# Second block of a two-block transformer: the dilated branch's projections placed around the latent norms and ahead of the up-projections

## What is computed

```python
h = rmsnorm(x, attn_norm[l])
c_q, c_kv, k_r, q_d, k_d, v_d = split(h @ w_in[l])      # 384, 256, 32, 512, 512, 512 columns
o_a = mla_mixer(c_q, c_kv, k_r, ...)                    # latent branch
    # q  = rmsnorm(c_q) @ w_uq   -> 8 heads x 96
    # kv = rmsnorm(c_kv) @ w_ukv -> 8 heads x (64 + 64)
    # per-head rmsnorm of q and k (96 wide), rope on the last 32, dense attention
o_b = dilated_attention(rmsnorm(q_d), rmsnorm(k_d), v_d, rel_bias)   # 8 heads x 64, per-head norm
x = x + concat(o_a, o_b) @ w_out[l]
x = x + conv_ffn(rmsnorm(x, ffn_norm[l]), ...)
```

## Time and profile before

| | |
|---|---|
| time, 3 runs | 2110.36, 2115.12, 2116.67 us, median 2115.12 |
| span of the profiled execution | 2111.4 us |
| its own time | not given apart from the span; the span lies 3.7 us below the median |
| busy: PE / PEld / DVE / ACT / POOL | 92% / 77% / 52% / 40% / 13% |
| mean granted TensorE clock | 0.953 |
| DMA | 254.93 MB, mean 121 GB/s |

### The profile page before, as it was taken

How to read it: one execution, slowest core, us unless ns; L and a number is a source line. 1 busy time by engine, 2 the same in 40 slices (tenths; PEclk the granted TensorE clock), 3 DMA queues, 4 the chain that set the end, 5 groups by cost and what they waited for, 6 DMA issues and landing times.

```text
span 2111.4 us, 31880 instructions
## 1 busy us (share of the span) xinstructions
PE 1948.4 (92%) x12326; PEld 1628.3 (77%) x12326; DVE 1107.7 (52%) x2071; ACT 843.1 (40%) x1579; POOL 283.1 (13%) x194
## 2 busy tenths in 40 slices
PE   5799999999999998998779997979899988799998
PEld 2595555758888887993379997867899987778998
DVE  0523433464344345334556556186687744858785
ACT  1323334343323234223434444345455434545453
POOL 1200000110000012100000001230323113213221
PEclk9899999999999999999889998889999988899999
DMA  9313333433333332413435663440465534224663
GB/s 271 110 61 120 112 108 120 139 91 99 97 98 95 100 99 91 120 61 129 129 83 160 184 181 102 123 125 1 122 190 172 157 90 145 81 61 138 180 182 100
DMA packets 405876, 254.93 MB, mean 121 GB/s; under 512 B 8064, under 2 KB 404640, under 8 KB 405728
## 3 DMA queue, kind: packets, MB, share of 16 engines
q1 hardware_dynamic: 404576, 249.19, 39.9%
q0 software_dynamic: 1152, 3.71, 0.7%
HBM read 251.75 MB, written 1.11 MB: 120 GB/s over the span
## 4 chain that ended last, share of the span: by engine, by line
PE 83%; DVE 9%; ACT 3%; issue 2%; DMA 2%; POOL 2%; SPq 0%; DVEq 0%; ACTq 0%; POOLq 0%
PE bank L1685 59%; PE bank L1664 8%; PE bank L1767 5%; PE bank L1784 5%; PE bank L1776 3%; DVE WORK L1453 2%; PE bank L1735 1%; DVE TOK L1594 1%; ACT parts L1055 1%; DMA raw<-ada_w 1%; PE bank L1762 1%; DVE parts L882 1%; POOL parts L882 1%; DVE TOK L1589 1%; POOL WORK L1007 1%
## 5 line engine op out<-in xcount | busy, mean ns | idle before, releaser
L1685 PE MATMUL bank<-AT,parts 128*128 128x256 f32 (+1 forms) x4656 | 689.6, 310 | 29.3 <-DVE AT L868 16.2
L1685 PEld LDWEIGHTS bank<-AT,parts 128*128 128x128 f32 x4656 | 639.0, 194 | 79.6 <-issue 29.6
L1055 ACT ACTIVATE parts<-raw 128x1024 fp32r<-128x1024 f32 (+1 forms) x368 | 368.1, 1040 | 327.8 <-PE bank L1685 316.3
L882 DVE TENSOR_TENSOR parts<-raw,parts 128x1024 fp32r<-128x1024 f32 (+2 forms) x300 | 416.0, 1412 | 151.7 <-ACT parts L1055 151.1
L1685 PE MATMUL bank<-HID,parts 128*128 128x256 f32 (+1 forms) x2592 | 399.8, 316 | 9.1 <-DVE HID L1401 9.1
L1685 PEld LDWEIGHTS bank<-HID,parts 128*128 128x128 f32 x2592 | 367.2, 192 | 39.9 <-DVE HID L1401 9.7
L1685 PE MATMUL bank<-parts,AT 128*128 128x256 f32 (+1 forms) x2208 | 285.0, 291 | 35.2 <-POOL parts L882 19.1
L1685 PEld LDWEIGHTS bank<-parts,AT 128*128 128x128 f32 x2208 | 279.2, 200 | 42.0 <-issue 28.5
L882 POOL TENSOR_TENSOR parts<-raw,parts 128x1024 fp32r<-128x1024 f32 x68 | 169.0, 2493 | 510.8 <-ACT parts L1055 510.6
L1664 PE MATMUL bank<-raw,CS 128*2 128x256 f32 x768 | 180.3, 390 | 22.4 <-DMA CON<-const 12.4
L1664 PEld LDWEIGHTS bank<-raw,CS 128*2 128x2 f32 x768 | 63.1, 86 | 126.3 <-issue 40.0
(11 more groups left out here) (145 smaller groups left out, 1360.0 us busy)
## 6 DMA issues: line engine op xcount, KB each, us to landing
raw<-mlp_w SPq DMA_DIRECT2D x128, 512.0 KB, 4.0
raw<-ada_w SPq DMA_DIRECT2D x96, 512.0 KB, 4.6
raw<-w_up SPq DMA_DIRECT2D x88, 512.0 KB, 4.7
raw<-w_in SPq DMA_DIRECT2D x32, 512.0 KB, 4.8
raw<-w_down SPq DMA_DIRECT2D x32, 512.0 KB, 4.0
raw<-odd_w_in SPq DMA_DIRECT2D x24, 512.0 KB, 3.6
raw<-w_out SPq DMA_DIRECT2D x16, 512.0 KB, 3.6
raw<-even_w_in SPq DMA_DIRECT2D x12, 512.0 KB, 4.1
```

Source lines behind the costliest of these rows:

```text
L882: ng.tensor_tensor(chunk_part(c, 1), chunk_raw(c), chunk_part(c, 0).bitcast(F32), ALU.subtract)\
L1055: return nc.scalar.activation(o, i, ACT.Copy)
L1685: ins = MM(out, stay, move, start=kt == 0 and i == 0, stop=kt == kts - 1 and i == 2)
```

## The change

In `plan()` the second block's layer gets another order:

- `dil` 0 stands directly behind the latent projections; then come `stat cq` and `stat ckv`; then `dil` 1, 2, 3; then the seven up-projections `mq` and `mkv`; then `dil` 4 and 5.
- the `post` units: `dq` behind `dil` 1, `dk` behind `dil` 3, `mq` behind the up-projections (ahead of `dil` 4), `mk` behind `dil` 4.
- the 4 `turn` units of the dilated branch come ahead of the 8 of the latent branch, and the jobs of kind N ahead of those of kind M.
- ACT squares the five latent tiles at the end of its part of `latent` 2, no longer in the two `stat` units; so it does that ahead of draining `dil` 0.

By the rule above the splits of the dilated chunks move too: those of `dil` 0 go behind `latent` 1, of `dil` 1 behind `latent` 2 (behind the squares), of `dil` 2 behind `stat ckv`, of `dil` 3 behind `dil` 1, the four chunks of `dil` 4 and 5 behind `mq` 1, `mq` 2, `mkv` 0 and `mkv` 1 (where those of `dil` 0 and 1 stood before). Those of `w_out_2` stay behind `dil` 4 and 5.

The rope tables of the first block shrink to one copy of a head's 64 columns: `CON` goes from 1744 to 976 columns. DVE reads them with a broadcast over the heads; the product with the sine is written as four instructions a unit, one for each half and block of tokens, where it was two.

```diff
@@ plan(), second block @@
         for n in range(3):
             pan = panel("w_in_2", l, 0, KT, n * PW, PW if n < 2 else 160)
             add("latent", ("latent", l, n), layer=l, n=n, panel=pan)
-        norm("cq", l, N, "g_cq", src="CQ", dst="CQ", kts=QLT)
-        norm("ckv", l, N, "g_ckv", src="CKV", dst="CKV", kts=KVT)
-        for n in range(3):
-            pan = panel("w_uq_2", l, 0, QLT, n * PW)
-            add("mq", ("mq", l, n), layer=l, n=n, panel=pan)
-        for n in range(4):
-            pan = panel("w_ukv_2", l, 0, KVT, n * PW)
-            add("mkv", ("mkv", l, n), layer=l, n=n, panel=pan)
         for n in range(6):
+            if n == 1:
+                norm("cq", l, N, "g_cq", src="CQ", dst="CQ", kts=QLT)
+                norm("ckv", l, N, "g_ckv", src="CKV", dst="CKV", kts=KVT)
+            if n == 4:
+                for m in range(3):
+                    pan = panel("w_uq_2", l, 0, QLT, m * PW)
+                    add("mq", ("mq", l, m), layer=l, n=m, panel=pan)
+                for m in range(4):
+                    pan = panel("w_ukv_2", l, 0, KVT, m * PW)
+                    add("mkv", ("mkv", l, m), layer=l, n=m, panel=pan)
+                add("post", ("post", l, "mq"), what="mq", layer=l)
             pan = panel("w_in_2", l, 0, KT, 672 + n * PW)
             add("dil", ("dil", l, n), layer=l, n=n, panel=pan)
-            for what in {0: ("mq",), 1: ("mk",), 3: ("dq",), 4: ("dk",)}.get(n, ()):
+            for what in {1: ("dq",), 3: ("dk",), 4: ("mk",)}.get(n, ()):
                 add("post", ("post", l, what), what=what, layer=l)
+        for part in "qk":
+            for i in range(2):
+                add("turn", ("turn", 2 + l, "d" + part, i), layer=2 + l, ft=("d" + part, i))
         for part in "qk":
             for i in range(4):
                 add("turn", ("turn", 2 + l, "m" + part, i), layer=2 + l, ft=("m" + part, i))
-        for part in "qk":
-            for i in range(2):
-                add("turn", ("turn", 2 + l, "d" + part, i), layer=2 + l, ft=("d" + part, i))
-        attention([job(kind=k, layer=2 + l, h=h, b=b, keys=256) for k in "MN" for h in range(8) for b in range(TB)])
+        attention([job(kind=k, layer=2 + l, h=h, b=b, keys=256) for k in "NM" for h in range(8) for b in range(TB)])
@@ ACT, unit "stat" @@
-                    if x.src != "H":
-                        settle()
                     for kt in range(x.squared, x.kts):
@@ ACT, unit "latent", n == 2 @@
+                        settle()
+                        for name in ("cq", "ckv"):
+                            st = index[("stat", name, x.layer)]
+                            for kt in range(st.kts):
+                                square(pos, st, kt)
@@ DVE, unit "tok" with rope @@
-                        step(V.tensor_tensor(pick(r, half), pick(src, 1 - half), pick(sin, half), ALU.mult))
+                        for tb in range(TB):
+                            sn = sin[:, tb:tb + 1, :, half, :].broadcast_to([P, heads, 2, 16])
+                            step(V.tensor_tensor(pick(r, tb, half), pick(src, tb, 1 - half), sn, ALU.mult))
...
```

More of the change, by code:

```diff
@@ L78 @@
 ROWS_W = _at
-CONST = {"ident": 0, "cos": 128, "sin": 128 + 512, "window": 128 + 1024, "near": 128 + 1024 + 384,
-         "inv_freq": 128 + 1024 + 384 + 64, "flip": 128 + 1024 + 384 + 64 + 16}
-CONST_W = 128 + 1024 + 384 + 64 + 16 + 128
+CONST = {}
+_at = 0
+for _name, _w in (("ident", P), ("cos", TB * HD), ("sin", TB * HD), ("window", 384), ("near", 64), ("inv_freq", 16),
+                  ("flip", P)):
+    CONST[_name] = _at
+    _at += _w
+CONST_W = _at
 def constants():
@@ L97, in constants @@
         rows = slice(b * P, (b + 1) * P)
-        c[:, 128 + b * PW:128 + (b + 1) * PW] = np.tile(np.cos(ang[rows]), (1, 4))
-        c[:, 640 + b * PW:640 + (b + 1) * PW] = np.tile(np.sin(ang[rows]) * sign, (1, 4))
+        c[:, CONST["cos"] + b * HD:CONST["cos"] + (b + 1) * HD] = np.cos(ang[rows])
+        c[:, CONST["sin"] + b * HD:CONST["sin"] + (b + 1) * HD] = np.sin(ang[rows]) * sign
     p = np.arange(P)[:, None]
@@ L107, in constants @@
     c[:, CONST["inv_freq"]:CONST["inv_freq"] + 16] = inv
-    c[:, CONST["flip"]:] = np.eye(P, dtype=f)[::-1]
+    c[:, CONST["flip"]:CONST["flip"] + P] = np.eye(P, dtype=f)[::-1]
     rel = np.arange(512) - 255
@@ L932, in two_block_kernel @@
                     x.squared = KT - per
+        for st in stats_by_n:
+            if st.src != "H":
+                st.squared = st.kts
         first = stats_by_n[0]
@@ L1470, in _, with pick @@
                     r = ROT[:, x.rot % 2, :].rearrange("p (t c) -> p t c", t=TB)
-                    cos = CON[:, CONST["cos"]:CONST["cos"] + 512].rearrange("p (t c) -> p t c", t=TB)
-                    sin = CON[:, CONST["sin"]:CONST["sin"] + 512].rearrange("p (t c) -> p t c", t=TB)
+                    cos = CON[:, CONST["cos"]:CONST["cos"] + TB * HD].rearrange("p (t c) -> p t c", t=TB)
+                    sin = CON[:, CONST["sin"]:CONST["sin"] + TB * HD].rearrange("p (t g h c) -> p t g h c", t=TB, g=2,
+                                                                               h=2)
+                    heads = cols // HD
                     for half in range(2):
-                        def pick(a, h):
-                            return a[:, :, 0:cols].rearrange("p t (g h c) -> p t g h c", h=2, c=16)[:, :, :, h, :]
-                        step(V.tensor_tensor(pick(r, half), pick(src, 1 - half), pick(sin, half), ALU.mult))
+                        def pick(a, t, h):
+                            return a[:, t, 0:cols].rearrange("p (n g h c) -> p n g h c", g=2, h=2, c=16)[:, :, :, h, :]
+                        for tb in range(TB):
+                            sn = sin[:, tb:tb + 1, :, half, :].broadcast_to([P, heads, 2, 16])
+                            step(V.tensor_tensor(pick(r, tb, half), pick(src, tb, 1 - half), sn, ALU.mult))
                     if cols == P:
@@ L1480, in _ @@
                     for tb in range(TB):
-                        ins = V.tensor_tensor(f(tb, x.n * PW, cols), src[:, tb, 0:cols], cos[:, tb, 0:cols], ALU.mult)
+                        ins = V.tensor_tensor(f(tb, x.n * PW, cols).rearrange("p (n c) -> p n c", c=HD),
+                                              src[:, tb, 0:cols].rearrange("p (n c) -> p n c", c=HD),
+                                              cos[:, tb:tb + 1, :].broadcast_to([P, heads, HD]), ALU.mult)
                         if tb == 0:
```

## The result

The changed kernel takes 2135.6 us (median of 4 runs, 2132.2 to 2140.4), the kernel before 2113.4 in the runs beside it (2110.4 to 2116.7): a ratio of 1.0103, with an interval of 1.0081 to 1.0126. That is **slower by 22 us**, where 16 less were forecast. The profiled execution has a span of 2130.4 us, 19.0 more than before, and a mean granted clock of 0.937 (before 0.953).

A forecast was written before the change was run, and what follows sets the result against it. It took the kernel as PE-bound, with gains only where PE stands still or runs at the lower clock. 8.1 + 7.8 - 2 times 0.5 + 1.1 = 16.0 us less than 2115.1 gave 2099 us, range 2090 to 2108.

The forecast's parts named there:

- Kind N first: Start of the attention: some three N jobs replace M jobs at half clock, costing 0.5 us per layer.
- a slow start of kind N: Start of the attention: listed as a sign that the prediction was wrong, with no size or chance given.
- C: Rival, chance 0.04: both wide norms meet POOL, costing 16.8 us per layer, so the kernel is slower at 2133 us.
- `dil` 0 in the first hole: After the latent matmuls: `dil` 0 starts without a hole, loses 2.0 us to half clock and ends at 7.9 us.
- The new hole ahead of `dil` 2: On PE between `dil` 1 and `dil` 2: a wait of 2.9 us for POOL's low parts.
- The up-projections: On PE behind `dil` 3: 14.9 us at full clock, where they took 16.91.
- The two wide norms alone: Stage's tail on DVE, without POOL beside it: 1.83 us a pair of products, the stage ending at 78.1 us.
- The tables: Start of the kernel: the smaller `CON` loads sooner, 1.1 us less before the weights PE waits for.
- A: Rival, chance 0.17: the lower clock and new hole cost little, 2.0 to 3.5 us less per layer, 2092 to 2095.
- B: Rival, chance 0.12: POOL's late low parts meet DVE's products in one wide norm, giving 2107 or 2116 us.
- D: Rival, chance 0.07: the order does nothing, as DVE is the bound both ways; 2113 us.

The follow-up runs named there:

- e1: The changed kernel with the jobs of kind M first again, the rest of the change kept: 2094.9 us, ratio 0.9915 to the kernel before.
- e2: The kernel before with the jobs of kind N ahead of those of kind M, nothing else: 2151.1 us, ratio 1.0179.
- e3: The kernel before with only the change's smaller rope tables and their products: 2111.0 us, ratio 0.9990.
- e6: The changed kernel with kind M first, and the low parts of the first two `w_out_2` panels on POOL instead of DVE: 2099.7 us, ratio 0.9945.
- e7: The changed kernel with four jobs of kind M, then all 16 of N, then the other twelve of M: median 2117.0 us, ratio 0.9996.
- e8: The changed kernel with one extra 256-column matmul in each of the first eight N jobs per layer: median 2145.2 us, ratio 1.0136.
- e5: The changed kernel with 12 extra dense matmuls ahead of the last turn in each layer: median 2125.3 us, ratio 1.0041.

## Why the prediction was wrong

**The step that failed is "Kind N first".** I put it at 0.5 us per layer, with bounds of nothing and 3 times 0.32, and it cost 17.5 and 16.4 us in the profiled run: all sixteen jobs of N ran at 1.2 GHz, not the first three. By the cross of e1 and e2 it is 19 to 20 us per layer. The working took the two kinds' job times from the earlier trace rows, both at a clock of 1.00, and assumed that the clock returns after a few microseconds of dense work, whichever kind that is. But in the kernel before N never had to bring the clock back: it ran behind M, which had done so. The earlier trace rows could not show what N does from 1.2 GHz, and a term whose row was taken in another state of the clock had no right to a bound of 1 us. The bound from the rows at hand would have been the whole of N at half pace: sixteen jobs times 1.44 at most, 23 us per layer, which turns a gain of 16 into a loss of 30. I listed "a slow start of kind N" among what would make the prediction wrong and gave it no price and no chance. None of the four rivals contained it; C ended on the right side, at 2133, near the 2135.6 measured, but that is luck: its mechanism did not happen.

**Everything else was close.** With the failed term taken out, the same sum is 17 us less, and e1 measured 17.5 less (13.7 to 22.2 by its interval). Some of that closeness is luck: the stage of e1 lasts 79.9 us in the first layer and 76.7 in the second, where 78.1 was forecast.
- *`dil` 0 in the first hole*: no hole, as forecast. The clock was away for less than I had: 0.59 and 0.55 in 1342 to 1346 and 1.00 from 1346, so about 1 us was lost in place of 2.0. That too varies: in e1's first layer, from 1337.39, the clock was at 0.50 until 1342 and at 1.00 only from 1344.
- *The new hole ahead of `dil` 2*: 2.94 us, forecast 2.9, released by POOL. Of DVE's scaling and POOL's low parts side by side, it was DVE that paid: two of those scalings took 5.00 us at 1358.78, against 1.28 for three alone at 1353.98, while POOL's four low parts took 9.99 (9.52 alone). So the hole is not the 0.5 us wider that the prediction feared from this, though the scaling was slowed by far more than double. The slow scaling cost nothing, since the up-projections that need it start at 1372.68. In e1's first layer the hole cost more than its length: behind it the clock fell to 0.50 in 1358 to 1360, and `dil` 2 and 3 took 13.25 us in place of 11.75.
- *The up-projections*: 14.84 us, forecast 14.9.
- *The two wide norms alone*: 1.83 us a pair, with 1.83 forecast, and the two pairs of low parts at 2.35. `post mq` ends on DVE at 1402.04, 58.8 us after the start (forecast 60.3), the copies end at 1420.0, 76.8 after it (forecast 78.1).
- *The tables*: in the kernel after, 0.5 us at the first matmul and 1.1 at the first norm's sums, as forecast; in e3, 1.1 at the first matmul and 0.1 at the sums. The 1.1 us of the sum is not shown.

**Of the rivals**, A was nearly true for the first microseconds (1 us less per layer than my walk), B and C did not occur, as no product of the wide norms met POOL, though e6 shows their price to be real. D falls: the stage got shorter by 9.0 and 9.3 us.

**What stays open.** Why kind N does not bring the full clock back. At 1.2 GHz PE's records are gapless in N as in M; the weight loads take 2.0 to 2.8 of 4 us in N and 3.6 in M, and N's scores have 64 rows where M's have 96. No run took these apart. Also open is why the second layer of e2 gained the clock and lost it again. The Trainium skill (TensorE: Matmul & The Clock Gate, "Part 1: The HAM clock gate") ties the full clock to sustained activity. That M brings it back agrees with that; that some 40 us of N without a gap (sixteen jobs of 2.62) do not is more than a busy PE in the profile lets one expect, and here the measurement decides.

## What to carry to other kernels

Where a stage begins after a stretch in which PE is nearly idle, look at what the first jobs are: put first the kind that has been seen to bring the granted clock from 0.50 to 1.00, and do not take a job's duration from a row at another clock. A reordering of equal work is not free in itself, and its bound is the whole reordered stretch at half pace. Look at every layer of a trace, and at more than one execution: e2 and e7 did two different things in their two layers. When a change bundles several edits, price each one's worst case, the smallest too: here it cost more than twice what the rest had won.

## What the runs showed of the hardware that was not expected

- **Kind N mostly keeps the clock that it finds.** It ran at 1.2 GHz for over 36 us with PE busy without a pause, in both layers of the kernel after, in the first of e2 and of e7 and, with the added matmuls, in the second of e8; in no trace did the clock rise later than N's first scores. Begun at 2.4 GHz, the same jobs stayed there (before, e1, e5, the second layer of e7), but for the second layer of e2, where the clock fell after 3.4 us.
- **Kind M brings it back, in its own time**: 2.1 and 6.0 us behind its first score in e1, 11.2 and 11.4 in e2. In e7's first layer four jobs of M (6.4 us) did not.
- **The outcome varies between executions of one program** when the work ahead of N is just enough or just not: two groups of runs about 20 us apart in e5, 2091 and 2117 in e7, 2120 and 2144 to 2149 in e8. Neither the change (2132 to 2140) nor e1 (2092 to 2100) shows such groups in its four runs.
- **DVE's scaling with two SBUF inputs and 256 columns** took 5.00 us for two beside POOL's low parts, 1.28 for three alone: about six times as long for each, more than the 3.3 times of the wide products in e6. Put per instruction the two are alike: a scaling lasted 2.50 us beside low parts of 2.50 each (9.99 for four), a wide product 3.04 beside low parts of 3.13 each (6.26 for two). So where POOL is at work all along, a DVE instruction lasts about as long as POOL's in these rows, and a small one pays relatively most; where POOL is there for a part of the time it is less (4.01 and 3.85 a pair in e6).
